# The head stream of a mixer stage: SP issues the spreading copies, values ahead of the second projected tile

## What is computed

```python
qa, ka, va, za, qb, kb, vb, zb = jnp.split(rms_norm(x, g) @ w_in, cuts, axis=-1)
# four heads of differential attention over all 1024 keys, with a distance bias
s1 = q1 @ k1.T * scale + bias;  s2 = q2 @ k2.T * scale + bias
oa = (softmax(s1) - lam * softmax(s2)) @ va
# eight heads of neighbourhood attention on a 16 x 64 grid, window 8 x 16, with rpb bias
ob = softmax(qb @ kb_near.T * scale + rpb_bias) @ vb_near
y = concat([rms_norm(oa) * silu(za), ob * silu(zb)]) @ w_out;  x = x + y
```

## Time and profile before

| | us |
|---|---|
| median of 3 runs | 3866.23 (3866.18 to 3867.72) |
| the profiled execution, its own time | 3857.56 |
| its span | 3855.8 |
| PE busy in the span | 3372.1 |
| mixers: start to first step / steps of units 0 to 6 / unit 7 | about 0 to 118 / 118 to 738 / 738 to 790 |

### The profile page before, as it was taken

The page is one execution under the profiler, slowest core; times in us unless marked ns, Lnnn a source line. Parts: engine busy times, 40 slices in busy tenths (PEclk is TensorE's granted clock), DMA queues, the critical chain, the costliest instruction groups (busy, mean ns, idle before and its releaser), DMA issues. The chain is left out here.

```text
span 3855.8 us, 51966 instructions
## 1 busy us (share of the span) xinstructions
PE 3372.1 (87%) x20036; PEld 2956.4 (77%) x20036; DVE 1740.5 (45%) x3202; ACT 838.6 (22%) x1622; POOL 1123.8 (29%) x716
## 2 busy tenths in 40 slices
PE   6999999998816789879999999559998979999996
PEld 5898898888815578868888888548887968888885
DVE  3646464524385533163333334535554263333336
ACT  2545454402101121021111111213333021111110
POOL 4434343321045422233223330300000253322322
PEclk8999999889956789989999999779999979999998
DMA  6011111311100011111111110100000121111111
GB/s 197 30 46 44 44 44 43 154 33 59 24 4 13 9 55 33 55 51 59 54 44 44 54 54 0 34 14 14 14 14 21 39 72 55 49 49 44 44 44 44
DMA packets 179259, 173.03 MB, mean 45 GB/s; under 512 B 50266, under 2 KB 162330, under 8 KB 178970
## 3 DMA queue, kind: packets, MB, share of 16 engines
q1 hardware_dynamic: 159902, 164.08, 13.1%
q10 hardware_dynamic: 19232, 7.23, 0.8%
HBM read 157.30 MB, written 19.23 MB: 46 GB/s over the span
## 5 line engine op out<-in xcount | busy, mean ns | idle before, releaser
L2000 DVE TENSOR_TENSOR x<-x,banks 128x512 f32<-128x512 f32 x512 | 343.8, 684 | 209.6 <-PE banks L80 209.6
L78 PE MATMUL banks<-winbuf_hi,xt_hi 128*128 128x256 f32 x1024 | 306.5, 299 | 38.0 <-ACT qkn L906 34.6
L79 PE MATMUL banks<-winbuf_lo,xt_hi 128*128 128x256 f32 x1024 | 294.2, 287 | 0.0
L80 PE MATMUL banks<-winbuf_hi,xt_lo 128*128 128x256 f32 x1024 | 294.1, 287 | 0.0
L78 PEld LDWEIGHTS banks<-winbuf_hi,xt_hi 128*128 128x128 f32 x1024 | 200.5, 196 | 57.0 <-issue 35.8
L78 PE MATMUL banks<-h1t_hi,f1w_buf_hi 128*128 128x512 f32 x512 | 200.0, 391 | 3.0 <-PEq L1926 3.0
L78 PE MATMUL banks<-h3t_hi,f2w_buf_hi 128*128 128x512 f32 x512 | 199.9, 390 | 2.8 <-PEq L1926 2.8
L79 PEld LDWEIGHTS banks<-winbuf_lo,xt_hi 128*128 128x128 f32 x1024 | 201.3, 197 | 0.0
L80 PEld LDWEIGHTS banks<-winbuf_hi,xt_lo 128*128 128x128 f32 x1024 | 200.7, 196 | 0.0
L80 PE MATMUL banks<-h3t_hi,f2w_buf_lo 128*128 128x512 f32 x512 | 199.9, 390 | 0.0
L79 PE MATMUL banks<-h1t_lo,f1w_buf_hi 128*128 128x512 f32 x512 | 199.8, 390 | 0.0
(11 more groups left out here) (417 smaller groups left out, 8869.4 us busy)
## 6 DMA issues: line engine op xcount, KB each, us to landing
f1w_raw<-in_w_ff SPq DMA_DIRECT2D x32, 1024.0 KB, 5.0
f2w_raw<-in_w_ff SPq DMA_DIRECT2D x32, 1024.0 KB, 5.0
winraw<-in_w_in SPq DMA_DIRECT2D x128, 128.0 KB, 3.3
gluw_raw<-in_ssm_w_glu SPq DMA_DIRECT2D x16, 512.0 KB
x<-in_x SPq DMA_DIRECT2D x8, 512.0 KB, 7.0
wow_raw<-in_w_out SPq DMA_DIRECT2D x4, 1024.0 KB, 5.1
x<-in_x SPq DMA_DIRECT2D x1, 4096.0 KB, 15.1
gew_raw<-in_w_ple_gate SPq DMA_DIRECT2D x4, 1024.0 KB, 5.0
```

What stands on the lines that cost most here:

```text
L78: nc.tensor.matmul(out, a.hi, b.hi, start=start, stop=False)
L79: nc.tensor.matmul(out, a.hi, b.lo, start=False, stop=False)
L80: return nc.tensor.matmul(out, a.lo, b.hi, start=False, stop=stop)
L2000: nc.vector.tensor_tensor(xx, xx, chip.ps[:, 4 + w % 4, :], ALU.add).then_inc(s_acc, 1)
```

## The change

1. PE: in each step `values(g)` comes before `project(n+1)`, no longer after it. `project(n+1)` is then followed at once by the next step's `project`, except where output or head transposes or scores stand between (t = 1, 4, 5, 6, 7).
2. ACT: `squares(g)` follows `evacuate(g)`, and `taken(n+1)` and the exponentials of g+2 come behind it. The sigmoid at t = 0 comes behind `taken(n)` and `evacuate(g)`. At t = 7 `taken(n)` and `evacuate(g)` come ahead of the exponentials.
3. DVE: in N units `finish(g-1)` is the first thing in a step.
4. SP issues the 16 `spread_edges` and three `spread_strip` copies, behind `strips(0)`; `edges(0)` moves behind the next four weight pieces.
5. The four lam vectors are loaded by SP behind the tiles of x, on a semaphore of their own; DVE's two reductions over them stand four tiles later, and PE's one-row matmul stands after tile 7 instead of tile 5.

```diff
@@ -544,6 +544,8 @@
                 weights(piece)
             for j in range(1, NT):
                 sp.dma_start(m.x[:, j, :], x_tok[:, j, :]).then_inc(s_xin[j], 16)
+            for n, name in enumerate(("lam_q1", "lam_k1", "lam_q2", "lam_k2")):
+                sp.dma_start(m.lamv[:, n, :], io[name]).then_inc(s_lam, 16)
             for n, name in enumerate(("q_norm_a", "k_norm_a", "q_norm_b", "k_norm_b")):
                 for h in range(2):
                     sp.dma_start(m.gains[64 * h:64 * h + 64, n:n + 1], io[name]).then_inc(s_gl, 16)
@@ -562,12 +564,18 @@
             for piece in range(8, 12):
                 weights(piece)
             strips(0)
-            edges(0)
+            sp.wait_ge(s_wide, 16)
+            for h in range(H_NA):
+                spread_edges(sp, h)
+            for n in range(1, H_DIFF):
+                spread_strip(sp, n)
             for u in range(NU - 1):
                 for t in range(4):
                     weights(4 * (2 * u + 3) + t)
                 if u:
                     store(u - 1)
+                else:
+                    edges(0)
                 if u < NU - 2:
                     for t in range(4):
                         weights(4 * (2 * u + 4) + t)
@@ -816,7 +824,7 @@
 
             pe.wait_ge(s_ident, 1)
             norm_transposes(0)
-            pe.wait_ge(s_load, 96)
+            pe.wait_ge(s_load, 32)
             for n in range(4):
                 distance_bias(n)
             pe.wait_ge(s_bv, 4)
@@ -829,7 +837,7 @@
                 project(j)
                 if j + 2 < NT:
                     norm_transposes(j + 2)
-                if j == 5:
+                if j == 7:
                     pe.wait_ge(s_const, 2)
                     pe.wait_ge(s_v, 4)
                     nc.tensor.matmul(chip.ps[:, 7, 0:1], m.onerow[:, :], m.lrow[:, :], start=True, stop=True).then_inc(s_cm, 1)
@@ -853,9 +861,9 @@
                     transposes(g)
                     if t < 6:
                         scores(g + 2)
+                    values(g)
                     if more:
                         project(n + 1)
-                    values(g)
                     if t == 1 and u:
                         out_transposes(u - 1, 1)
                     if t == 4:
@@ -950,10 +958,8 @@
                 nc.scalar.activation(token_cols(dst, q), chip.ps[:, 4, :].rearrange("p (c r) -> p c r", r=NT),
                                      ACT.Copy).then_inc(s_yh, 1)
 
-            for n, name in enumerate(("lam_q1", "lam_k1", "lam_q2", "lam_k2")):
-                act.dma_start(m.lamv[:, n, :], io[name]).then_inc(s_load, 16)
+            act.dma_start(m.hot[:, :], io["c_onehot"]).then_inc(s_load, 16)
             act.dma_start(m.table[:, :], io["t5_bias"]).then_inc(s_load, 16)
-            act.dma_start(m.hot[:, :], io["c_onehot"]).then_inc(s_load, 16)
             row_squares(0)
             norm_hi(0)
             row_squares(1)
@@ -974,14 +980,6 @@
                     norm_hi(j + 2)
                 if j + 4 < NT:
                     row_squares(j + 4)
-                if j == 4:
-                    act.wait_ge(s_wide, 16)
-                    for h in range(H_NA):
-                        spread_edges(act, h)
-                if j == 6:
-                    act.wait_ge(s_bst, 16)
-                    for n in range(1, H_DIFF):
-                        spread_strip(act, n)
             act.wait_ge(s_gs, 3)
             for n in range(NT, 2 * NT):
                 taken(n)
@@ -999,33 +997,34 @@
                 for t in range(NT):
                     g, n = NT * u + t, 2 * NT * (u + 1) + 2 * t
                     more = u < NU - 1
+                    if more:
+                        taken(n)
+                    evacuate(g)
                     if t == 0:
                         act.wait_ge(s_gate, 2 * u)
                         nc.scalar.activation(m.sig[:, :, :], m.vz[:, u % 2, :, P:2 * P], ACT.Sigmoid).then_inc(s_sig, 1)
-                    if more:
-                        taken(n)
-                        if t == 7:
-                            expo(g + 1, 0)
-                    evacuate(g)
-                    if more and t == 7:
+                    if t < 7:
+                        squares(g)
+                        if more:
+                            taken(n + 1)
+                        if t < 6:
+                            expo(g + 2, 0)
+                        if t == 1 and u:
+                            out_hi(u - 1, 1)
+                        if t == 4:
+                            out_hi(u, 0)
+                        if more and t in (5, 6):
+                            head_hi(u + 1, 2 * (t - 5))
+                            head_hi(u + 1, 2 * (t - 5) + 1)
+                        if t < 6:
+                            down(g + 2)
+                            expo(g + 2, 1)
+                    elif more:
+                        expo(g + 1, 0)
                         down(g + 1)
+                        taken(n + 1)
                         expo(g + 1, 1)
-                    if more:
-                        taken(n + 1)
-                    if t < 6:
-                        expo(g + 2, 0)
-                    squares(g)
-                    if t == 1 and u:
-                        out_hi(u - 1, 1)
-                    if t == 4:
-                        out_hi(u, 0)
-                    if t < 6:
-                        down(g + 2)
-                        expo(g + 2, 1)
-                    if more and t in (5, 6):
-                        head_hi(u + 1, 2 * (t - 5))
-                        head_hi(u + 1, 2 * (t - 5) + 1)
-                    if more and t == 7:
+                        squares(g)
                         expo(g + 2, 0)
                         down(g + 2)
                         expo(g + 2, 1)
@@ -1160,10 +1159,6 @@
             norm_lo(0)
             for n in range(4):
                 distance_bias(n)
-            dve.wait_ge(s_load, 96)
-            for n in range(2):
-                nc.vector.tensor_tensor_reduce(m.prod[:, n, :], m.lamv[:, 2 * n, :], m.lamv[:, 2 * n + 1, :], 1.0, 0.0,
-                                               ALU.mult, ALU.add, m.lsum[:, n:n + 1]).then_inc(s_v, 1)
             normalise(1)
             normalise(2)
             head_sums(0)
@@ -1172,6 +1167,10 @@
             head_scale(0)
             normalise(3)
             normalise(4)
+            dve.wait_ge(s_lam, 64)
+            for n in range(2):
+                nc.vector.tensor_tensor_reduce(m.prod[:, n, :], m.lamv[:, 2 * n, :], m.lamv[:, 2 * n + 1, :], 1.0, 0.0,
+                                               ALU.mult, ALU.add, m.lsum[:, n:n + 1]).then_inc(s_v, 1)
             head_sums(1)
             norm_lo(3)
             head_scale(1)
@@ -1201,14 +1200,14 @@
                 for t in range(NT):
                     g, a = NT * u + t, NT * (u + 1) + 2 * t
                     more = u < NU - 1
+                    if not dense and g:
+                        finish(g - 1)
                     if more and t < 4:
                         head_sums(a)
                     if more and 1 <= t <= 4:
                         head_scale(a - 1)
                     if more and t == 7:
                         biased(g + 1)
-                    if not dense and g:
-                        finish(g - 1)
                     evacuate(g)
                     if dense and g:
                         finish(g - 1)
```

More of the change, by code:

```diff
@@ L479, in stage_mixers @@
         s_sst = sems(nc, ctx, "mxst", "0 1 2 3")
-        (s_load, s_const, s_ident, s_pad, s_rpb, s_wide, s_bst, s_gl, s_gs, s_xg, s_v, s_e, s_cm, s_bv, s_sed) = sems(
-            nc, ctx, "mxc", "load const ident pad rpb wide bst gl gs xg v e cm bv sed")
+        (s_load, s_const, s_ident, s_pad, s_rpb, s_wide, s_bst, s_gl, s_gs, s_xg, s_v, s_e, s_cm, s_bv, s_sed, s_lam) = sems(
+            nc, ctx, "mxc", "load const ident pad rpb wide bst gl gs xg v e cm bv sed lam")
         (s_xs, s_xe, s_xp, s_xn, s_xt, s_xh, s_xl) = sems(nc, ctx, "mxn", "xs xe xp xn xt xh xl")
```

## The result

| | before | after |
|---|---|---|
| median, us | 3866.2 (3863.95 to 3867.72, 6 runs) | 3882.55 (3875.14 to 3889.5, 6 runs) |
| ratio | | 1.0043, 95% interval 1.0027 to 1.0059 |
| the profiled execution, its own time | 3857.56 | 3887.53 |
| T of unit 0, step 0 starts at | 114.47 | 88.66 |
| units 0 to 6 (T of unit 0 to T of unit 7) | 621.6 | 672.4 |

The changed kernel is slower by 16.3 us. The sum had 15, the forecast was 3881. The trace splits the difference as the prediction did: the start gives 25.8 us, the steps of units 0 to 6 take 50.8 back (41 in the prediction), unit 7 gives 2.3, and at the end of the stage after is 22.7 us behind. The two profiled executions differ by 30 us.

A forecast was written before the change was run, and what follows sets the result against it. PE is busy for 3372.1 of 3855.8 us, so its waits and order decide. The terms -26 + 26 + 22 + 1 + 9 - 21 + 4 = +15 on 3866.2 gave 3881 us, range 3847 to 3897.

The forecast's parts named there:

- Start: Projection start: with the copies on SP, tile 8 starts at 53.9 instead of 78.98; gain 26 us.
- Two tiles back to back: Steps of units 0 to 6: P1 follows P2 at once and waits for ACT; cost 26 us.
- V behind S: Steps t = 6 and 7: V, with less cover, waits for evacuations and finish; cost 22 us.
- the clock: D and N t = 7: the granted clock falls after some of PE's new waits; cost 4 us.
- D t = 0: Units 2, 4, 6 at t = 0: V waits about as long as P2 did before; 0 us.
- ACT's chain in D units: D units, t = 1 and 2: exponentials start at the step's end, so V waits on ACT's chain; cost 9 us.
- Gains: In the steps: finish first in N units, the later sigmoid and earlier high parts remove waits; gain 21 us.
- 1 (V hardly waits): Steps: evacuations come sooner, V's waits total under 15 us; sum -20, 3846 us, faster; chance 0.22.
- 2 (the chain and the clock cost nothing): Steps: waits at t = 6 and 7 are real, ACT's chain and clock free; +2, 3868 us; chance 0.16.
- 3 (late weights): First split: weight pieces 12 to 15 land after 110 and POOL stands; +10 more, 3891 us; chance 0.09.
- 5: Start: no gain, the stall goes over to the DMA or POOL; +41, 3907 us; chance 0.05.
- 4 (clock at every wait): Steps: the clock falls at every new wait; +8 more, with some chain losses 3893 us; chance 0.10.

The follow-up runs named there:

- e1: The kernel before with parts 4 and 5 of the change alone; 3841.8 us, ratio 0.9931.
- e11: The kernel before with part 4 alone, the lam vectors left on ACT's queue; 3843.52 us, ratio 0.9947.
- e5: The changed kernel with ACT copying a query/key tile out of bank 6 first and squaring the copy; 3894.35 us, ratio 1.0076.
- e4: The changed kernel with the values back behind the second projected tile at t = 6 and 7; 3850.91 us, ratio 0.9954.
- e3: The kernel before with parts 4 and 5 and, of the steps, part 3 alone; 3829.23 us, ratio 0.9895.
- e6: The changed kernel with the exponential's table loaded under P2 at D t = 0 and POOL's roots ahead of the gates; 3873.06 us, ratio 1.002.
- e2: The kernel before with parts 1, 2 and 3 alone, the copies left on ACT; 3915.1 us, ratio 1.0119.
- e10: The changed kernel with POOL's roots ahead of the gates and nothing else; 3883.09 us, ratio 1.0041.

## Why the prediction was right, and where not

- **Start, -26**: right, -25.8 in the trace and -25.1 alone (e1). By the traces 0.8 of it is the lam vectors' (e11). The Trainium skill ("DMA: Bandwidth & Descriptors", Issuing engines are not separate DMA queues) says that starting DMAs from several engines saves only the sequencer's time, usually small beside the DMA. The first half agrees with e1; the time was not small here, with ACT's queue held for 20.91 us by fifteen copies, and PE waited for ACT.
- **Two tiles back to back, +26**: right. 28 waits, 19.0 us idle. From the last matmul of P2 to the first of P1 it takes 0.9 more than without a wait at t = 0 and 2, 1.0 at t = 3, 0.55 at t = 1 and 0.3 at t = 4 behind the transposes: 26 in all. What the prediction did not see is that in D units ACT's chain is just as long (e5).
- **V behind S, +22, and the clock, +4**: the mechanism was right, the size was not. This is the term that was mis-sized: 36.9 us by steps, 31.6 by medians, clock included (e4). The waits themselves came as predicted: at t = 6 and 7 they add up to 22.0 (2.57 for 2.4 at N t = 7; 1.81 for 1.9 at D t = 7), and as steps without clock they cost 23.5. Two things were not in the term. The late end of N t = 7 costs 1.75 at each next t = 0, 5.2 in all, for which I had nothing. And the clock fell by 1.5, 1.5 and 3.1 at the three N t = 7, and by 2.9 at D t = 0 and 2.1 at D t = 7 of unit 6, 11.1 in all, where I had set 4; 2.9 of it doesn't show in the difference, since a slow P2 shortens V's wait at the next t = 1 (1.18 for 2.46 in unit 6) and e4's trace has a fall of its own.
- **D t = 0, 0**: 14.15 became 14.37 in units 2 and 4, as forecast, but by luck of the clock. Before's 14.15 holds a fall behind the 2.40 wait of the earlier trace rows; in e3 the same wait has none, and the step takes 12.65. There t = 1 is 1.2 longer, so the fall cost 0.3 over the two steps and not the 1.7 read from the earlier trace rows.
- **V in the middle D steps, +1**: hardly there, V starts at most 0.1 later.
- **ACT's chain in D units, +9**: right in sum (8.9 at t = 1 in e6) and mostly in place (+3.0 in units 2, 4, 6 for 2.6; in unit 0 +2.4, bank term included). That the order of roots and gates on POOL holds 1.1 of the 2.5 was not seen.
- **Gains, -21**: near. `finish` first gave 12.6 (10.4 predicted), the high parts 1.0 to 1.2 at D t = 5, the first step of unit 7 3.8 (2.65 predicted). Working back: 26 + 36.9 + 8.9 less 50.8 leaves 21 in units 0 to 6, where the prediction had 18 and the 2.65 of unit 7.
- The sum +15 against +22.7 at the stage's end is the miss of the V term and the clock, less what the gains gave more. That the median's +16.3 is nearer to the forecast than the trace is luck: it lies between two groups of executions, about 11 and 22 us above before.
- **Rivals.** 1 (V hardly waits) fell with the 22.0 us of waits at t = 6 and 7, where it allowed 15, and with e4, 2 (the chain and the clock cost nothing) with e6 and the row of 463:468. 3 (late weights) fell with POOL's row at 100.25; the pieces stood behind the copies, and had the time. 5 fell with e1. 4 (clock at every wait) was half right: at N t = 7 three times of three and at D t = 0 and 7 of unit 6, but not at the waits of 2.61 and 2.46 at D t = 0 and 1 of unit 4 (478.12, 491.83).

What stays open: a second place for projected tiles, which would take away P1's wait for the bank and nothing else, wasn't tried; seven banks are taken, and the other half of bank 6 would be written by PE while ACT reads the first. The first step of unit 0 gained 0.46 and not 1.8: V waits there 2.07 for ACT's evacuation, in place of P2, and the clock fell behind it (0.72 over 94:100). In e2 the same step took 14.58 without a fall, and t = 1 14.24 for 12.64, so that the two together are 28.8 in both; this trade between a step and the next is seen, and not explained in full.

## What to carry to other kernels

A move that shortens one wait shifts cover: list what each neighbour of the moved block was hiding, and price it at the steps where nothing else stands between. A change of several parts is best priced and run by parts: here the copies (-25) and `finish` first (-13) were worth 38 us, and lost to a reordering of PE and ACT that cost some 60 (by the sum of e2 and e3; it wasn't run alone). When a late item (the sigmoid) is moved back, follow it through every in-order queue that has something else behind its consumer; here that was POOL, and two swapped lines were worth 10 us by medians and 8 by steps.

## What was not expected of the hardware

Waits of PE of the same length cost different clock. Behind 2.57 us at 461.48 the granted clock was 0.66 over 5 us, a mix of the 2.4 and the 1.2 GHz level. Behind 2.61 us at 478.12 it was 1.00 (the 2.4 GHz level), and behind 2.60 us at 669.04 0.50 (the 1.2 GHz level) for 4 us. Rows of the windows, as above, the granted clock behind the count in brackets:

```profile
478.00:484.00 6.00, 5.13 (x42) 1.00 0.01 3
...
669.00:673.00 4.00, 3.96 (x18) 0.50 0.02 4
```

Nor does the same place always cost the same. The 2.57 of N t = 7 stands in five kernels (after, e2, e5, e6, e10), fifteen times in their traces: the clock fell behind it twelve times, and three times not (step 13.03). The 1.81 of D t = 7 cost nothing in units 0, 2 and 4 of after, and 2.1 in unit 6. The 1.74 at N t = 2 and 3 cost nothing in before, and 1.5 or so at four places in e11. So neither the length of a wait nor the place tells its price in clock from one trace; it has to be read in several.
